# A hybrid decoder step on one core: own buffers for the recurrence's last group, sums of squares one block sooner, half of the weight sums beside the latent queries

## What is computed

```python
# the recurrence, per chunk (64 heads in 8 groups)
decay = exp(where(causal, cum_i - cum_j, -inf))
y = einsum('bijge,bjgep->bigep', decay * cb, xdt) + (C . s) * exp(cum)
s_new = s * exp(last) + einsum('bjge,bjgep,bjgn->bgepn', w_end, xdt, B)
y = rmsnorm_by_group((y + xs * D) * silu(z)) * gate_norm ;  x = x + y @ w_out
# the attention layer
kv = [rmsnorm(a[..., :512]), rope(a[..., 512:])],  a = rmsnorm(x) @ w_kv_a
r  = rsqrt((|rows[:512] @ w_uk|^2 + |rows[512:]|^2) / 192 + eps)      # per key and head
q_lat = q[:128] @ w_uk^T ;  s = (q_lat . rows[:512] + q_rope . rows[512:]) * r
o = (softmax(s) @ rows[:512]) @ w_uv ;  x = x + (o * silu(gate)) @ w_out
```

## Time and profile before

| | |
|---|---|
| median of 3 runs | 2373.68 us |
| the profiled execution | 2373.9 us, its span 2372.1 us |
| mean granted clock of TensorE | 0.972 |
| TensorE, matmuls | 2228.7 us busy, 94% of the span |
| VectorE | 1348.9 us, 57% |
| ScalarE | 1112.7 us, 47% |
| GpSimd | 1077.8 us, 45% |
| DMA | 309.83 MB, 131 GB/s on the mean |

### The profile page before, as it was taken

One profiled execution on the slowest core, in us unless ns is written; L12 is line 12 of the kernel. 1 busy time (PEld: TensorE's weight loads), 2 busy tenths in 40 slices (PEclk: granted clock), 3 DMA queues, 4 the chain that ended last, 5 costly groups with the idle time before them and its releaser, 6 DMA issues. The chain is left out here.

```text
span 2372.1 us, 39390 instructions
## 1 busy us (share of the span) xinstructions
PE 2228.7 (94%) x13958; PEld 1903.2 (80%) x13958; DVE 1348.9 (57%) x2187; ACT 1112.7 (47%) x2840; POOL 1077.8 (45%) x712
## 2 busy tenths in 40 slices
PE   6999999999999998799999986999999999999689
PEld 5989898989888987589997764777777777777489
DVE  4766676767676767552126656565555565655410
ACT  4455545454545454543344534554444444545222
POOL 5565656565555655156760005433333333333065
PEclk8999999999999999799999987999999999999899
DMA  4564646464646464234442312212202112022444
GB/s 155 200 222 162 230 167 219 171 216 169 226 163 228 168 217 160 99 128 158 152 151 108 111 57 79 66 31 61 70 22 71 33 52 68 25 66 61 191 151 138
DMA packets 80349, 309.83 MB, mean 131 GB/s; under 512 B 14578, under 2 KB 21874, under 8 KB 54690
## 3 DMA queue, kind: packets, MB, share of 16 engines
q1 hardware_dynamic: 80162, 307.38, 38.5%
HBM read 279.56 MB, written 27.79 MB: 130 GB/s over the span
## 5 line engine op out<-in xcount | busy, mean ns | idle before, releaser
L671 POOL TENSOR_TENSOR w_lo<-raw,w_hi 128x1024 fp32r<-128x1024 f32 x218 | 540.8, 2501 | 363.0 <-ACT w_hi L861 362.9
L122 PE MATMUL bank<-h_hi,w_hi 128*128 128x304 f32 x1776 | 552.3, 311 | 25.4 <-POOLq L254 13.5
L124 PE MATMUL bank<-h_hi,w_lo 128*128 128x304 f32 x1776 | 538.3, 303 | 0.0
L123 PE MATMUL bank<-h_lo,w_hi 128*128 128x304 f32 x1776 | 536.1, 302 | 0.0
L122 PE MATMUL bank<-b_hi,a_hi 128*128 128x512 f32 x896 | 363.3, 406 | 26.8 <-issue 15.0
L861 ACT ACTIVATE w_hi<-raw 128x1024 fp32r<-128x1024 f32 x216 | 216.6, 1050 | 350.3 <-PE bank L124 350.3
L122 PEld LDWEIGHTS bank<-h_hi,w_hi 128*128 128x128 f32 x1776 | 335.8, 189 | 41.2 <-POOLq L254 13.7
L123 PE MATMUL bank<-b_lo,a_hi 128*128 128x512 f32 x896 | 356.5, 398 | 0.0
L124 PE MATMUL bank<-b_hi,a_lo 128*128 128x512 f32 x896 | 356.0, 397 | 0.0
L123 PEld LDWEIGHTS bank<-h_lo,w_hi 128*128 128x128 f32 x1776 | 337.0, 190 | 2.3 <-issue 1.7
L124 PEld LDWEIGHTS bank<-h_hi,w_lo 128*128 128x128 f32 x1776 | 336.2, 189 | 0.0
(11 more groups left out here) (368 smaller groups left out, 3943.1 us busy)
## 6 DMA issues: line engine op xcount, KB each, us to landing
raw<-in_a_units SPq DMA_DIRECT2D x112, 1024.0 KB, 5.0
raw<-in_b_in_units SPq DMA_DIRECT2D x20, 1024.0 KB, 4.9
past<-in_cache SPq DMA_DIRECT2D x64, 288.0 KB, 3.3
s_in<-in_state_in SPq DMA_DIRECT2D x32, 512.0 KB, 6.9
s_t<-in_state_t SPq DMA_DIRECT2D x16, 1024.0 KB, 6.3
out_state_out<-s_in SPq DMA_DIRECT2D x32, 512.0 KB, 6.8
pt<-in_cache_t SPq DMA_DIRECT2D x64, 256.0 KB, 2.6
raw<-in_o_units SPq DMA_DIRECT2D x16, 1024.0 KB, 5.1
```

The costliest lines, as they stand in the source:

```text
L122: nc.tensor.matmul(out, a[0], b[0], start=start, stop=False)
L123: nc.tensor.matmul(out, a[0], b[1], start=False, stop=False)
L124: return nc.tensor.matmul(out, a[1], b[0], start=False, stop=stop)
L671: nc.gpsimd.tensor_tensor(w_lo[u % 2][:, c], raw[u % 2][:, c], w_hi[u % 2][:, c].bitcast(F32), ALU.subtract).then_inc(lo_done, 1)
```

## The change

There are four edits. **(A)** The eighth group's decays 2 to 7, its cum rows for pairs 2 and 3, the second half of s_t and its last quarter of states get tiles of their own, which lie over h_hi and h_lo. SP loads the latter four kinds together as soon as block xC is done. The last group's pieces get an order of their own on each engine. **(B)** In the trunk the last two sums of squares both stand behind kv block 0 (KV0). **(C)** The high and low parts of the first halves of products 0, 1 and 4, and the first halves of three sums, are made in q_lat_stage; sample_attention_stage makes the remaining ones in a new order. w_uv and the attention's output are loaded some products later. **(D)** The first two output weights are loaded near the end of sample_attention_stage, and ScalarE takes the pieces of the value stage in another order.

```diff
+    last = Space(nc, s.at)
     put("h_hi", [P, KT, TOK], F32R)
     put("h_lo", [P, KT, TOK], F32R)
+    for e in range(2, HPG):
+        m[f"dec_last{e}"] = last(f"dec_last{e}", [P, PAIR_N])
+    for p in range(2, PAIRS):
+        m[f"cum_last{p}"] = last(f"cum_last{p}", [P, 2, TOK])
+    m["s_t_last"] = last("s_t_last", [P, 4, GW])
+    m["s_last"] = last("s_last", [P, PAIRS, 2, STATE])
+    assert last.at <= s.at
...
+    dec_at = lambda g, e: m[f"dec_last{e}"] if g == LAST and e >= 2 else dec[e % 2]
+    cum_at = lambda g, p: m[f"cum_last{p}"] if g == LAST and p >= 2 else cumb[p % 2]
+    state_at = lambda n: m["s_last"] if n == LAST_STATE else s_in[n % S_RING]
...
+    TURNED = DENSE[at["o", LAST - 1, KT - 2] % 2]
...
+            def last_group_in():
+                block_wait(sp, "c", LAST, xC)
+                sp.dma_start(m["s_t_last"][:], d["state_t"][LAST, 1]).then_inc(t_last_in, 16)
+                for p in range(2, PAIRS):
+                    src = d["cum"][LAST * HPG + 2 * p:LAST * HPG + 2 * p + 2, :].rearrange("e t -> (e t)").partition_broadcast(P)
+                    sp.dma_start(m[f"cum_last{p}"][:].rearrange("p e t -> p (e t)"), src).then_inc(cum_last_in[p], 16)
+                sp.dma_start(m["s_last"][:], d["state_in"][LAST, 3]).then_inc(s_last_in, 16)
+
+            def last_group_out():
+                for q in range(3):
+                    state_out(4 * LAST + q)
+                sp_out(LAST)
+                state_out(LAST_STATE)
+
             def start(g, n):
+                if n == 0 and g == LAST:
+                    last_group_in()
...
-                if n == 3:
+                if n == 3 and g < LAST:
...
                     of_states(g, 0)
+                    if g == LAST:
+                        of_states(g, 1)
...
+            def last_heads():
+                pair_y(LAST, 0)
+                pair_y(LAST, 1)
+                states_turned(LAST)
+                update(LAST, 1)
+                pair_y(LAST, 2)
+                prompt_state(LAST)
+                pair_y(LAST, 3)
+                update(LAST, 2)
+                squares(LAST)
+                update(LAST, 3)
...
+                if g == LAST and p:
+                    block_wait(act, "c", LAST, xC)
+                else:
+                    y_done.wait(act, g if p else g - 1, p - 1 if p else PAIRS - 1)
...
                 if n == 2:
                     e_cum(g)
                     decay(g, 0)
+                    if g == LAST:
+                        decay(g, 1)
                 if n == 3:
-                    decay(g, 1)
+                    if g == LAST:
+                        decay(g, 2)
+                        decay(g, 3)
+                        states_back(g)
+                    else:
+                        decay(g, 1)
+
+            def last_heads():
+                for e in range(4, HPG):
+                    decay(LAST, e)
+                split(LAST_UNIT + 1)
+                for p in range(PAIRS):
+                    square(LAST, p)
+                root(LAST)
+                y_high(LAST, 0)
+                y_high(LAST, 1)
...
+                if g == LAST and e >= 2:
+                    nc.vector.tensor_tensor(dc[0:48, 0:304], dc[0:48, 0:304], m["cb"][0:48, 0:304], ALU.mult)
+                    nc.vector.tensor_tensor(dc[:, 304:688], dc[:, 304:688], m["cb"][:, 304:688], ALU.mult).then_inc(mix_done.sem, 1)
+                else:
+                    nc.vector.tensor_tensor(dc[:], dc[:], m["cb"][:], ALU.mult).then_inc(mix_done.sem, 1)
...
+                if g == LAST and c >= 14:
+                    mix(g, c - 14)
+
+            def last_heads():
+                mix(LAST, 2)
+                mix(LAST, 3)
+                add_y(LAST, 0)
+                update(LAST, 0)
+                mix(LAST, 4)
+                mix(LAST, 5)
+                add_y(LAST, 1)
+                add_states(LAST)
+                mix(LAST, 6)
+                mix(LAST, 7)
+                add_y(LAST, 2)
+                gated(LAST, 0)
+                gated(LAST, 1)
+                gated(LAST, 2)
+                update(LAST, 1)
+                add_y(LAST, 3)
+                gated(LAST, 3)
+                update(LAST, 2)
+                scaled(LAST, 0)
+                scaled(LAST, 1)
+                y_low(LAST, 0)
+                y_low(LAST, 1)
+                prompt_state_back(LAST)
+                update(LAST, 3)
...
-                if c in (KV0, KV0 + 1):
-                    sum_of(c - 2)
+                if c == KV0:
+                    sum_of(KT - 2)
+                    sum_of(KT - 1)
...
+                if c == 8:
+                    for of, value in stored:
+                        dve.wait_ge(of, value)
...
+            for n in EARLY:
+                if n == 4:
+                    act.wait_ge(kept["o_out"], 16 * Q_PAIRS)
+                act.wait_ge(kept["uk_in"][n == 4], 16)
+                nc.scalar.activation(flat(m[f"b_hi{n}0"]), right[n][0], ACT.Copy).then_inc(first_high, 1)
...
+            def first_low(n):
+                dve.wait_ge(first_high, high_base + EARLY.index(n) + 1)
+                nc.vector.tensor_tensor(flat(m[f"b_lo{n}0"]), right[n][0], flat(m[f"b_hi{n}0"]).bitcast(F32), ALU.subtract).then_inc(first_b, 1)
+
+            def rows_of(k):
                 dve.wait_ge(ql_done, done_base + k + 1)
                 nc.vector.tensor_copy(m["ql_rows"][:, k, :], psum[k][:, :]).then_inc(ql_out, 1)
+            first_low(0)
+            rows_of(0)
+            first_low(1)
+            rows_of(1)
+            dve.wait_ge(kept["uk_in"][1], 16)
+            dve.wait_ge(first_b, b_base + 1)
+            nc.vector.tensor_tensor(b11[0], b12[0], b11[0], ALU.subtract).then_inc(first_b, 1)
+            rows_of(2)
+            rows_of(3)
+            first_low(4)
+            dve.wait_ge(first_b, b_base + 3)
+            nc.vector.tensor_tensor(b12[0], b22[0], b12[0], ALU.subtract).then_inc(first_b, 1)
+            dve.wait_ge(first_b, b_base + 5)
+            nc.vector.tensor_tensor(b22[0], b22[0], b11[0], ALU.subtract).then_inc(first_b, 1)
...
-    B_HI = (0, 1, 4, 2, 3, 5, 6)
+    b11, b12, b21, b22, right, flat = right_sides(m)
...
-            k_done.wait(sp, last, ended + 3)
+            k_done.wait(sp, last, ended + 5)
             sp.dma_start(m["w_uv"][:], d["kv_units"].rearrange("(u w) p n -> w p u n", w=2)[1]).then_inc(kept["uv_in"], 16)
-            for half, product in enumerate((5, 13)):
+            for half, product in enumerate((10, 13)):
                 k_done.wait(sp, last, ended + product)
                 heads = slice(8 * half, 8 * half + 8)
                 sp.dma_start(m["o"][:, heads, :], d["o_kept"][:, heads, :]).then_inc(kept["o_in"], 16)
+            s_done.wait(sp, last, PAGES - 1)
+            first.load(sp)
...
             def first_sums():
-                for n in (0, 1):
-                    for g in range(2):
-                        right_low(n, g)
-                for g in range(2):
-                    dve.wait_ge(kept["uk_in"][2 * g + 1], 16)
-                    b(nc.vector.tensor_tensor(b11[g], b12[g], b11[g], ALU.subtract))
-                for g in range(2):
-                    right_low(4, g)
+                right_low(0, 1)
+                right_low(1, 1)
+                dve.wait_ge(kept["uk_in"][3], 16)
+                b(nc.vector.tensor_tensor(b11[1], b12[1], b11[1], ALU.subtract))
+                right_low(4, 1)
+                right_low(2, 0)
 
             def second_sums():
-                for g in range(2):
-                    b(nc.vector.tensor_tensor(b12[g], b22[g], b12[g], ALU.subtract))
-                for g in range(2):
-                    dve.wait_ge(b_hi, 2 * B_HI.index(4) + g + 1)
-                    b(nc.vector.tensor_tensor(b22[g], b22[g], b11[g], ALU.subtract))
-                for g in range(2):
-                    right_low(2, g)
+                b(nc.vector.tensor_tensor(b12[1], b22[1], b12[1], ALU.subtract))
+                b(nc.vector.tensor_tensor(b22[1], b22[1], b11[1], ALU.subtract))
+                right_low(2, 1)
                 for g in range(2):
...
-            low_part(early, new, 2)
-            low_part(late, slice(0, TOK), 3)
+            low_part(late, prompt, 2)
+            low_part(slice(0, KT), new, 3)
...
             first.high(act, 0)
+            act.wait_ge(v_done, done_base + 4)
+            nc.scalar.activation(m["h_hi"][:, late, prompt], m["o"][:, late, prompt], ACT.Copy).then_inc(high, 1)
             first.high(act, 1)
             act.wait_ge(v_out, out_base + 4)
-            nc.scalar.activation(m["h_hi"][:, early, new], m["o"][:, early, new], ACT.Copy).then_inc(high, 1)
-            nc.scalar.activation(m["h_hi"][:, late, :], m["o"][:, late, :], ACT.Copy).then_inc(high, 1)
+            nc.scalar.activation(m["h_hi"][:, :, new], m["o"][:, :, new], ACT.Copy).then_inc(high, 1)
```

(21 more changed lines are left out.)

109 lines of the change are left out of this document (65 added, 44 removed).

## The result

The changed kernel takes 2345.73 us (median of 4 runs, 2340.48 to 2347.73) against 2374.2 for the kernel before; the ratio is 0.9879, with an interval of 0.9867 to 0.9891. So 28.5 us went, where the forecast had 33.7 and 2340.0 (range 2333 to 2353). The profiled execution has a span of 2345.9 us, 26.2 less than before; it was the longest of the four.

A forecast was written before the change was run, and what follows sets the result against it. Only long idle stretches of TensorE, where engines wait on each other, were taken to give much. Gains 16.8 + 1.9 + 8.5 + 6.5 = 33.7 us off 2373.9 give 2340.2, median 2340.0; range 2333 to 2353.

The forecast's parts named there:

- the first rival: Recurrence's tail: the clock falls all the same and TensorE sets the time; gain 9.8 instead of 16.8, 2347.0 us; chance 0.27.
- What is left is VectorE's list: Recurrence's tail: with decays made ahead, VectorE's instructions alone set its length, 25.4 us behind 939.0; gain 16.8 us.
- The clock: Recurrence's tail: a pair's matmuls take 1.55 us at full clock, or 2.78 us at the lower one.
- The price of GpSimd beside VectorE: Recurrence's tail: two mixes beside GpSimd take 4.20 us instead of 1.76, so 2.4 us more.
- The end: Tail to trunk: 1.5 us from VectorE's last instruction to the next stage's first matmul, 0.35 of it for a store.
- the forecast of 28.0: Recurrence's tail: from the end of out block 15 to the trunk's first matmul 28 us instead of 46.
- the later start: Sampled sequences' attention: VectorE's added sums beside the latent queries make GpSimd begin at 1437.0 instead of 1434.71, 2.3 us lost.
- The next pair's operands stand behind these on GpSimd: Attention entry: TensorE waits for operands behind GpSimd's low parts, so it follows their earlier end; gain 8.5 us.
- The reordered pieces: Value stage: ScalarE starts at 2241.2, takes the pieces in a new order and ends at 2250.0; gain with early loads 6.5 us.
- The rival on the slower side: Last out blocks: four early loads delay weight unit 108 and s_t; 40 us of stall gives 2380; chance 0.03.

The follow-up runs named there:

- filled: Changed kernel plus 12 matmuls whose results nobody reads, in two TensorE waits of the recurrence's tail; 2344.76 us, ratio 0.9883 to the kernel before.
- late_state: Changed kernel with the prompt's state moved behind the squares and last update on TensorE, and behind the last update on VectorE; 2344.23 us, ratio 0.9886.
- split_moved: Changed kernel with ScalarE's two halves of weight unit 109 apart, behind decay 5 and behind the third square; 2344.96 us, ratio 0.9886.
- all_three: Changed kernel with the prompt's state late, ScalarE's split in two places and 36 filling matmuls at six places in the tail; 2339.42 us, ratio 0.9852.
- no_tail: Changed kernel with only the recurrence's edit (last group's own buffers, loads and order) taken back; 2357.48 us, ratio 0.9934 to the kernel before.
- five_parts: Changed kernel with one of GpSimd's six low parts of the weight sums (product 3, second half) moved to VectorE; 2345.23 us, ratio 0.9882.
- units_old_order: Changed kernel with the output weights still loaded early but the value stage's pieces in the old order; 2345.81 us, ratio 0.9874.
- the second profile: The changed kernel, unaltered, timed and profiled again beside the kernel before; 2345.28 us, ratio 0.9879.
- late_and_moved: Changed kernel with the prompt's state late and ScalarE's split of unit 109 in two places, no filling; 2344.43 us, ratio 0.9881.
- filled_value: all_three plus 38 filling matmuls in the value stage, where TensorE stands still ahead of the dense stage; 2338.38 us, ratio 0.9844.

## Why the prediction was right, and where it was off

The direction, the order of the four gains and the range held. Term by term:

(A) Forecast 16.8, with the first rival at 9.8; measured 13.9 in the first profile and 12.2 by taking it back. The step that was off is "What is left is VectorE's list". It was VectorE's list and TensorE's at nearly the same length: in the first profile VectorE waited 3.0 us (0.39 and 1.79 for TensorE, 0.86 for the root behind the squares), where the sum had no wait at all. Three sizes were wrong.

The clock: I gave it two levels for the whole tail; it was at half for 10 to 14 us in the middle in both profiles of the changed kernel (my rival's mechanism, at about half its size).

The price of GpSimd beside VectorE: forecast 2.4 us, measured 3.25 (1.21 and 2.04 over the short durations), in two instructions, each held for most of one GpSimd half of 2.35. The Trainium skill ("SBUF — State Buffer", section "SBUF: two separate sides") says that the shared port pair is held for the whole instruction, and the trace agrees: each of the two halves held up one short VectorE instruction until about its own end. By that rule I had put the price at 5.3 us; it was less, since the first half was 1 us old (945.35) when VectorE's first instruction with two SBUF inputs came (946.35), and one of the two victims was an addition of 128 columns, not a mix.

The end: forecast 1.5, measured 1.67 (967.12 to 968.79).

What the runs show in place of the step: putting off the clock's fall alone (filled), moving TensorE's 5.8 us alone (late_state) or moving GpSimd's halves alone (split_moved) changes nothing. In split_moved the reason is shown: VectorE's list is shorter and it waits 4.20 us for TensorE. In the other two the waits on VectorE grew, but the clock's fall also reached the squares, so that the other list is as long is only in part what they show. All three together, with more filling, bring 4.2 to 4.9 us in the tail and 6 in the time. In all_three the clock was full and the interference was 1.2 us (one gate of 1.72 us), in place of 3.25: 26.6 plus the missing 2.0 is 28.6, an estimate, 0.6 over the forecast of 28.0. So most of the 3.4 us by which the tail exceeded the forecast (31.45 for 28.0) goes with the clock and the place of the prompt's state, which these runs don't part.

(B) Forecast 1.9, in the trace 2.1, bound by VectorE as forecast. It was not timed alone; the three others leave 1.0 for it. The profile of no_tail, which has B and not A, shows 1.9 between the two places.

(C) Forecast 8.5 with the later start taken off, in the trace 7.3 (8.7 from the stage's first sum on, less 1.4), taken back 7.3. GpSimd's end was forecast 32 us behind its first sum and was 33.6, and the stage began only 1.4 us later than it would have, not 2.3, since the six added instructions took 1.22 us each, without GpSimd beside them. But the reason was wrong in one step: "The next pair's operands stand behind these on GpSimd, and TensorE waits for them, so it follows." In the changed kernel it doesn't: five_parts shortens GpSimd's list by 2.5 us and gains 0.5. Most of the gain is in TensorE's two long waits, which the trace of before shows as

```profile
1441.46 0.77 PE L122 MATMUL bank<-b_hi,a_hi 128*128 128x512 f32 x1 [9.90 <-DVE b_lo L2527]
1459.85 0.77 PE L122 MATMUL bank<-b_hi,a_hi 128*128 128x512 f32 x1 [9.77 <-issue]
```

The first is 8.26 us now. The second ended as VectorE's b_lo of the earlier trace rows at 1458.53 ended its first half, and is 6.17 us now, with 1.42 behind it; the 1.5 us of short waits for GpSimd behind it (0.20, 0.67 and 0.66) are gone.

(D) Forecast 6.5, measured 6.4 and 7.4. The mechanism, the transfer, was right. The reordered pieces, of which I worked out a sum, have no part in it (units_old_order).

The rival on the slower side did not come: no matmul ahead of the out blocks 13 to 15 waited for a weight or for s_t.

The miss in the time is 5.7 us, and there are two accounts of it. By the trace the four parts are 4.0 short (A 2.9, C 1.2, B and D even), 3.5 were given back elsewhere, and 2.0 go off because the profiled execution was that much above the median: 5.5, and 0.2 more by which the forecast stood below its sum. By taking back, A is 4.6 short, C 1.2 and B 0.9, and D is 0.9 over: 5.8, with nothing left for the rest of the kernel. The runs don't decide between them, but A is the largest term in both. I had put no term for the clock outside the tail into the sum, though the earlier trace rows showed its mean at 0.77 and 0.72 in two stretches. One profile can't tell its usual share: the changed kernel's runs had a mean clock of 0.976 to 0.980.

## What to carry to other kernels

When a ping-pong between two engines is broken up, work out both lists of the stretch, not only the longer. Here they were close, and none of the three single edits showed a gain; the kernel with both lists shortened and TensorE filled did. Where TensorE waits within a stretch, its clock is part of the price, and matmuls without a reader in those waits can be worth more than they cost (5.0 us here, with filling in six places; nothing with filling in two). Read all waits of a stretch before naming its bound: the last releaser of an entry isn't what most of its idle time waits for.

## What the runs showed of the hardware

The granted clock fell around short waits. In the tail of the first profile it was at half from 942 on, behind waits of 1.37 and 0.57 us and although TensorE was then busy throughout. Behind the same two waits the second profile kept it at full until 946.5, where a wait of 0.94 us stood, and late_and_moved lost it between the two: one kernel's fall moves by some us from execution to execution. With 12 filling matmuls in those two waits (one profile) it stayed at full until 951. In the value stage it fell within a wait of 2.6 us behind 4.79 us of filling. With the tail filled at six places it stayed at full in all_three; in filled_value, with the same tail, it fell for 3.4 us just behind the trunk's start. In the 10 runs of the two kernels with the tail filled at six places the mean clock was 0.980 to 0.984; in the 8 of the changed kernel 0.976 to 0.980.

A VectorE product of 48 x 304 from two SBUF tiles took 2.50 us beside GpSimd's halves, and an addition of 128 x 128 1.50 to 1.98, where they take 0.46 and 0.29 alone; GpSimd in turn took 8.12 us for two halves beside VectorE's subtractions of 2176, 2176 and 512 columns, instead of 4.66. State updates with one input in PSUM, beside GpSimd in split_moved, kept their 2.15 us.
